# The starts of the large SBUF buffers in a two-block fp32 layer: 32-byte multiples, or 512-byte multiples

## The reference, cut to what matters

```python
h = rmsnorm(x, g_mix) @ w_in                      # 2048 -> 5,728 columns
...                                               # scan (1024 wide) and attention (1024 wide)
x = x + concatenate([y_ssd, y_att]) @ w_out       # 2048 -> 2048
u = rmsnorm(x, g_mlp) @ w_up                      # 2048 -> 8192
x = x + square(relu(u)) @ w_down                  # 8192 -> 2048
# second block
h = fox_attention(rmsnorm_2(x, norm_g[0]), fox_w_in, fox_b_f, fox_w_out)   # 2048 -> 6144 + 16, and 2048 -> 2048
x = x + rmsnorm_2(h, norm_g[1])
h = sqrelu_mlp(rmsnorm_2(x, norm_g[2]), mlp_w1, mlp_w2)                   # 2048 -> 8192 -> 2048
x = x + rmsnorm_2(h, norm_g[3])
```

## The kernel before, in words

| buffer | before | after |
|---|---|---|
| wh | 16512 (128) | 68096 (0) |
| X, CHx | 51680 (480) | 18944 (0) |
| XHL, TH | 68064 (480) | 35328 (0) |
| TL | 74208 (480) | 41472 (0) |
| raw and wl | 100832 (480) | 100864 (0) |
| hh / hl | 149984 / 182752 (480) | 150016 / 182784 (0) |
| CHb, HB, FQ | 133600 (480) | 133632 (0) |
| FK / FV / PTf | 149984 / 166368 / 182752 (480) | 32 bytes higher (0) |
| NHm / NLm | 161824 / 167968 (32) | 32 bytes higher (64) |
| NHf / NLf | 166368 / 167392 (480) | 32 bytes higher (0) |
| E, Vm, Q, K, PTm, Y | (32) | 32 bytes higher (64) |
| QT, KTt, V, KIT, QI | (192) | 32 bytes higher (224) |
| ident | 49280 (128) | 16512 (128) |

## Time and profile before

### The profile page before, as it was taken

One profiled execution on the slowest core, in us unless ns is written; L12 is line 12 of the kernel. 1 busy time (PEld: TensorE's weight loads), 2 busy tenths in 40 slices (PEclk: granted clock), 3 DMA queues, 4 the chain that ended last, 5 costly groups with the idle time before them and its releaser, 6 DMA issues. The chain is left out here.

```text
span 2265.9 us, 27606 instructions
## 1 busy us (share of the span) xinstructions
PE 2232.0 (99%) x11798; PEld 1899.8 (84%) x11798; DVE 1313.1 (58%) x1541; ACT 990.0 (44%) x1117; POOL 26.4 (1%) x71
## 2 busy tenths in 40 slices
PE   9999999999999999999999999999999999999998
PEld 8988778988888888887898888888888888888876
DVE  5688664555544466776455554546555444667754
ACT  6453554444433344544344434534445333444432
POOL 1000000000000000000001000000000000000000
PEclk9999999999999999999999999999999999999999
DMA  7455445566555566665557555555765556666664
GB/s 240 148 168 167 140 137 192 173 186 188 189 192 193 187 186 186 188 202 178 180 167 213 163 181 161 174 189 162 215 194 188 185 187 189 191 191 190 193 235 148
DMA packets 280985, 415.46 MB, mean 183 GB/s; under 512 B 13284, under 2 KB 167056, under 8 KB 280608
## 3 DMA queue, kind: packets, MB, share of 16 engines
q1 hardware_dynamic: 279376, 409.89, 56.5%
q0 software_dynamic: 1456, 3.81, 0.7%
q10 hardware_dynamic: 32, 0.01, 0.0%
HBM read 409.47 MB, written 4.21 MB: 183 GB/s over the span
## 5 line engine op out<-in xcount | busy, mean ns | idle before, releaser
L1123 DVE TENSOR_TENSOR wl<-raw,wh 128x2048 fp32r<-128x2048 f32 x376 | 860.2, 2290 | 494.8 <-ACT wh L605 493.3
L605 ACT ACTIVATE wh<-raw 128x2048 fp32r<-128x2048 f32 x376 | 719.4, 1916 | 531.4 <-DMA raw<-in_mlp_w_dram 169.5
L2012 PE MATMUL bank<-XHL,wh 128*128 128x512 f32 x2368 | 829.9, 393 | 0.0
L2014 PE MATMUL bank<-XHL,wl 128*128 128x256 f32 x2368 | 666.4, 281 | 0.0
L2012 PEld LDWEIGHTS bank<-XHL,wh 128*128 128x128 f32 x2368 | 444.2, 188 | 99.7 <-issue 0.2
L2014 PEld LDWEIGHTS bank<-XHL,wl 128*128 128x128 f32 x2368 | 446.0, 188 | 0.4
L1985 PE MATMUL bank<-wh,hh 128*128 128x512 f32 x768 | 301.9, 393 | 5.1 <-DVE wl L1123 5.1
L1987 PE MATMUL bank<-wh,hl 128*128 128x512 f32 x768 | 303.4, 395 | 0.0
L1986 PE MATMUL bank<-wl,hh 128*128 128x512 f32 x768 | 303.3, 395 | 0.0
L1985 PE MATMUL bank<-wh,XHL 128*128 128x512 f32 x576 | 231.2, 401 | 1.3 <-DVE XHL L1131 1.3
L1987 PE MATMUL bank<-wh,XHL 128*128 128x512 f32 x576 | 228.3, 396 | 0.0
(11 more groups left out here) (396 smaller groups left out, 1832.4 us busy)
## 6 DMA issues: line engine op xcount, KB each, us to landing
raw<-in_mlp_w_dram SPq DMA_DIRECT2D x128, 1024.0 KB, 5.4
raw<-in_w_up_dram SPq DMA_DIRECT2D x64, 1024.0 KB, 5.5
raw<-in_w_down_dram SPq DMA_DIRECT2D x64, 1024.0 KB, 5.1
raw<-in_fox_w_in_dram SPq DMA_DIRECT2D x48, 1024.0 KB, 5.4
raw<-in_w_in_dram SPq DMA_DIRECT2D x40, 1024.0 KB, 5.0
raw<-in_w_out_dram SPq DMA_DIRECT2D x16, 1024.0 KB, 5.1
raw<-in_fox_w_out_dram SPq DMA_DIRECT2D x16, 1024.0 KB, 5.1
raw<-in_w_in_dram SPq DMA_DIRECT2D x16, 256.0 KB, 6.9
```

The costliest lines, as they stand in the source:

```text
L605: act.activation(wh[:, j, :, :], raw[:, j, :, :], ACT.Copy).then_inc(hi_ready, 1)
L1123: dve.tensor_tensor(wl[:, j, :, :], raw[:, j, :, :], wh[:, j, :, :].bitcast(F32), ALU.subtract)\
L2012: pe.matmul(bk[:, :].rearrange("p (s t) -> p s t", s=2), sh, XHL[:, k, :, :], start=k == 0, stop=False, skip_group_check=True)
L2014: mm = pe.matmul(bk[:, 0:TOK], sl, XH[:, k, :], start=False, stop=k == KT - 1, skip_group_check=True)
```

## The change

Every large buffer begins at a multiple of 512 bytes. The arena's start is rounded to that, and `wh` moves from the front of memory into the arena, behind `XHL`, since the allocator would not have put it on such a multiple. The sizes of the buffers that follow are multiples of 512 for the large ones, so they keep the property; behind the small tables of the mixers it is lost, as the table above shows. `XHL` and `X` move down by some 33,000 bytes to the place that `wh` leaves, and all behind `wh` moves up by 32 bytes. No instruction is added, removed, changed in shape or put elsewhere: on every engine the same instructions stand in the same order with the same waits.

```diff
+LINE = 512
...
-        wh = sb("wh", [P, 4, 4, 512], F32R)
...
-        arena = -(-nc.sbuf_base // 32) * 32
+        def lined_up(at):
+            return -(-at // LINE) * LINE
+
+        arena = lined_up(nc.sbuf_base)
...
         arena = region(arena, [("XHL", [P, KT, 2, TOK], F32R)])
-        X, XHL, TH, TS, TL = (T[n] for n in "X XHL TH TS TL".split())
+        arena = region(arena, [("wh", [P, 4, 4, 512], F32R)])
+        X, XHL, TH, TS, TL, wh = (T[n] for n in "X XHL TH TS TL wh".split())
```

## The result

The changed kernel takes 2254.07 us in the median of six runs (2250.18 to 2255.22), the kernel before 2266.60 on the same chip (2263.44 to 2267.94): a ratio of **0.9944**, with 0.9932 to 0.9957 as its 95% interval. That is 12.5 us less where 54 were forecast. The profiled execution took 2253.77 us, its span is 2252.0 against 2265.9.

A forecast was written before the change was run, and what follows sets the result against it. TensorE was taken as the bound: matmul count times distance between starts. From 2267.7 us, 55.4 gained by settled distances (25.9 + 22.3 + 7.2) and 0.5 lost gave 2213 us, range 2195 to 2272 at 0.80.

The forecast's parts named there:

- Term 1, row form: Row form and `three`: with starts alike within 512 bytes, 4620 matmuls go from 232.3 to 226.7 ns, gaining 25.9 us.
- Term 1, pairs and full column form: 2368 half-panel pairs go from 349.4 to 340.0 ns (22.3 us); full column form from 118.0 to 113.3 (7.2 us).
- settled pair of 340 ns: Half-panel form: expected distance of a 512- and 256-column pair, 340.0 ns, from settled distances of 226.7 and 113.3.
- Terms 2 to 5: Weight splitting, loads into raw, fp32 products, x, constants and MLP scratch: nothing, save 0.5 us for waits on weights.
- No change: Rival, chance 0.22: the start is not the cause, as fp32 rows and wh as streamed operand suggest; 2267 us.
- The surplus goes altogether: Rival, chance 0.08: alignment also removes the sixteenth over the columns, 215.9 ns for 512; 146.5 us gained, 2121 us.
- Slower: Rival, chance 0.12: starts on a 64-byte multiple, as wh has, are the costly ones; 133 us lost, 2401 us.
- the likeliest case: All these products settle everywhere, between 2200 and 2245 us for a part settling late or not; chance 0.58.
- the 16-byte line: SBUF accesses are cheap within 16 bytes; all starts are multiples of 16, so nothing changes: 2267 us.

The follow-up runs named there:

- e1: Kernel before with wh alone moved up 352 bytes, to 480 past a multiple of 512, old buffer order kept: 2255.7 us, ratio 0.9953.
- e2: Changed kernel with its whole arena 32 bytes lower, large buffers all 480 past a multiple of 512, new order: 2256.4 us, ratio 0.9951.
- e3: Changed kernel's buffer order with the starts of the kernel before (wh 128 past a multiple of 512, the others 480): 2271.2 us.
- e5: Changed kernel with XHL, TH and TL 64 bytes past a multiple of 512, all else on multiples: 2254.6 us.
- e16: Changed kernel with XHL, TH and TL 192 bytes past a multiple of 512: 2252.7 us.
- e7: Changed kernel with everything behind raw (hh, hl, combinations, NHm, NLm and the rest) 32 bytes higher: 2271.1 us.
- e14: Changed kernel with each streamed operand of the row form cut into two halves of 256 columns: 2304.7 us, 120.2 ns a matmul.
- e13: Changed kernel with the half-panel form's second matmul widened from 256 to 512 streamed columns: 2483.2 us.
- e8: Changed kernel with raw and wl alone 32 bytes past a multiple of 512: 2262.0 us.

## Why the prediction was right and wrong

**What bounds the kernel.** Right: the difference between the spans is the count of matmuls times the distance of their starts, and TensorE's longest sorts of wait changed by at most 0.6 us.

**Term 1, row form.** Forecast 25.9 us from 5.6 ns on 4620 matmuls, measured 25.4. The reading of the earlier trace rows, that what `TH` has and `wh` has not is a common rest, is shown by e1, e2 and e3: undone with the new order of buffers it goes, done with the old order it comes. But the prediction took the rest by 64 for the common property, and that is too short: in e5 the two starts differ by 64 bytes, and the row form on XHL slows to 233.3. For TH, hh and wl, which all have 480, it made no difference which period was meant.

**Term 1, pairs and full column form.** This is the step that failed: "if it is the mixture that costs, all of these products settle". Forecast a gain of 22.3 and 7.2 us, measured a loss of 8.3 and 3.1. Two sources gave it. The settled pair of 340 ns was put together from the 226.7 of the seven-product slots and the narrow product's 113.3, and neither came from a place with this form's loads and streams. And the narrow product, which gave 113.3 ns for 256 columns, differs from the column forms in two ways. The first is its weights of 96 columns. The weight loads of the changed kernel show the difference:

```profile
L2016 PEld LDWEIGHTS bank<-XHL,wh 128*128 128x128 f32 x2368 | 445.9, 188 | 110.1 <-issue 0.2
...
L2247 PEld LDWEIGHTS bank<-XHL,NHm 128*96 128x96 f32 x16 | 2.6, 161 | 0.0
```

161 ns against 188. This alone does not decide: e16 and e5 have stretches at 113.3 with 128 weights. The second is the offset. NHm has 32 and XHL 480 by 512; they agree by 64, as the prediction says, but not by 256. Since NHm's slices follow each other at 384 bytes, XHL less NHm is 192 and 64 in turn, modulo 256, before the change and after it, and never 0. The changed kernel's narrow product settles as before (31 steps of its second half):

```profile
61.71 0.28 PE L2248 MATMUL bank<-XHL,NHm 128*96 128x256 f32 x1
...
65.22 0.28 PE L2249 MATMUL bank<-XHL,NLm 128*96 128x256 f32 x1
```

So it is in the traces of all ten kernels of this document in which the offset is 192 and 64 in turn, and in none of the eight others is there a settled stretch: e7, which moves NHm by 32 bytes, has 117.2, near the 117 that was expected. The full column form has offsets of 64 and 192 in e5 and e16, and there alone it was seen at 113.3. So the row that the prediction took for a settled product at a common start was one at offsets of 64 and 192, and the change gave the column forms the offset 0, at which 128 weights with 256 columns run at 120.0 (the full column form and e14) and a pair at 353.3. The traces show this pattern; no kernel was made to test it. It is not the whole rule either: with 192 about half of the full column form stayed at 117.8, and the pairs stayed at 353.3. And the product with 16 weight columns, which the prediction held against its reading, has slices every 64 bytes and so goes through four offsets, the same ones before and after; it took 117.2 ns before, 113.3 in the changed kernel, and 117.2 again in e13, which has the changed kernel's starts.

**Terms 2 to 5.** Right: 1916 and 2290 ns to the nanosecond, no wait grew by more than some tenths of a us, the fp32 forms did not move.

**The rivals.** 'No change' rested on the observation that wh as streamed operand was no faster than wl; true, and it is the mixture that slowed both (e8). 'The surplus goes altogether': no start that was tried brought the row form below 226.7, so the sixteenth over 213.3 is no matter of these starts. That leaves the 215.8 ns of the Trainium skill, "TensorE: Matmul & The Clock Gate", Back-to-back issue gap, unmet by this format in every run here. 'Slower' named the wrong culprit (e1 and e2 have no large float32r buffer on a multiple of 64, the changed kernel has them all there, and all three have the same distances), but its sign holds for the column forms, which it charged at +9.5 and +28.2 ns and which lost 2.0 and 3.5. A rival was missing: that one placement helps one form and harms another, with the net near zero.

The time lay in the range of 2195 to 2272, but outside the 2200 to 2245 of the likeliest case; the forecast of 54 us was four times too large. That it lay in the range is luck: the range reached so far up for the case of no change, and here a gain of about half the forecast size met a loss that was not forecast. The estimate made from the 16-byte line of the Trainium skill, "SBUF — State Buffer", Specifications (TRN2), by which nothing would change since all starts are multiples of 16, is not borne out: 32 bytes moved a distance by 6.6 ns.

## What to carry to other kernels

When matmuls follow each other with fresh weights each time and TensorE is the bound, measure the distance from start to start, form by form, and compare it with the fastest stretch of the same form; a few ns on ten thousand matmuls are per cents, and they can hang on how the start of the streamed buffer stands to that of the weights, within 256 bytes. A multiple of 512 for everything is not the aim: in this kernel it was right for 512 columns beside 128 weights and wrong for 256, so give each buffer its own rest and weigh the forms by their counts. Carry a distance over from one form to another only if the offset modulo 256 (slice by slice), weight columns, streamed columns and the neighbour's length are the same. And go through the whole trace: a form can run at two distances in one run, and one stretch shows only one of them.

## What the runs showed of the hardware that was not expected

- The distance of float32r matmuls depends on the streamed start less the weights' start, modulo 256 bytes: for 512 columns 226.7 ns at 0 and 228.8 to 234.3 at the seven other multiples of 32. For 256 columns beside 128 weights it was 120.0 at 0, and 113.3 was seen only at 64 and 192. That two reads of SBUF disturb each other is the likely reading; no run shows the reads themselves. The Trainium skill, "TensorE: Matmul & The Clock Gate", Step-by-step: what each phase is for, has loading the next weights take no read bandwidth from the running matmul; if the likely reading holds, that is not so for float32r. Nor is it settled why 32 and 160 are the best for the pairs.
- It runs in cycles that repeat for tens of matmuls, with VectorE, ScalarE and the DMAs at work beside them, and the same starts can hold two cycles in one run: 353.3 and 346.7 for the changed kernel's pairs, 117.8 and 113.3 for the full column form with `XHL` at 192. What picks the cycle is open. A neighbour of another kind changes all members: beside a 256-column matmul a 512-column one takes 236.7 ns, beside one of its own kind 226.6.
- For 512 columns no placement came below 17/16 of 213.3 ns, the time of 512 columns at 2.4 GHz, and for 256 columns none below 113.3, which is 17/16 of 106.7.
